# LSTM gates of one layer in one stationary block of 40 columns, and one gate row computed later

## The chip, the cores and the metric

The kernel runs on one core of a Trainium2 chip. The metric is the device time of one execution in microseconds (us). The kernel before took 2526.57, 2529.31 and 2533.30 us in three runs; the median is 2529.31 us.

## What is computed

A sequence of 256 positions with 1024 channels goes through a first block of two layers (band attention, short convolution, a gated feed-forward), and then through a second block of two layers. The first layer of the second block holds an mLSTM mixer, the second a stick-breaking attention, and both end in a "PEER" layer that picks 16 of 16384 experts for each of 8 heads and position and gathers their rows from memory. The change touches the gates of the mLSTM and the output gate of the first expert layer:

```
proj = einsum('bsd,de->bse', h, w_in)
qk, v, o, gates = split(proj, [1024, 2048, 3072])      # gates: 2 x 8 heads = 16 columns
gates = gates + b_if
i_pre, f_pre = split(gates, 2)                         # input gates, forget gates
log_f = log_sigmoid(f_pre);  b = cumsum(log_f)         # then the state and the decay of every head
...
sh1, sc1, g1, sh2, sc2, g2 = split(ada_mod(c), 6)      # per layer
x = x + g1 * mixer(h1)
x = x + g2 * peer_ffn(h2)                              # g2 of layer 0 is the gate row that moves
```

All arrays are float32.

## The kernel before, in words

Every engine has a program of its own, written out by hand, and the engines wait for each other on named semaphores. TensorE (PE) multiplies, VectorE (DVE) does most elementwise work, ScalarE (ACT) does activations, casts and copies out of PSUM, SyncE (SP) issues the weight loads, GpSimd (POOL) issues the gathers of expert rows. Nothing is scheduled by a planner at this place: the order of the work is the order of the code, and tables of small numbers say at which head or expert row an extra piece stands.

**The LSTM part.** The normed input is kept in two parts, `x_hi` and `x_lo` (the tiles `flo_b` and `hT_r` in the profile), and so are the weights; a product is three matmuls for each of 8 blocks of 128 channels (high by high, high by low, low by high). The gate weights are `wg`, split by ACT into `wg_hi` (L1734) and by DVE into `wg_lo` (`wg_r` in the profile, L2417). On PE the order is: values and queries and keys, then the gate product into bank `pr[0]` (twice 24 matmuls, input gates and then forget gates, each with 8 stationary columns), then four pieces of the output-gate product (`gate_piece`, 96 matmuls in line L647), then four small transposes of the gate rows (L1199) that wait for the semaphore `if_exp`, five matmuls that keep the engine at work (`idle_products_in`, L745), and then the heads, which wait for `gcol_ready`.

DVE meanwhile convolves queries and keys (`lstm_conv`), splits weights (`lower`, L1971), and when its program comes to L2451 it waits for the gate product (`if_full`), adds the biases into `gi` and `gf`, and runs the scans that give the cumulated decays. Behind the scans stand `lower(10)` and `lower(11)`, and behind these the copy `gcol` (L2473) that lets the heads begin.

**The heads.** In each of 8 heads PE multiplies `gM` (L1211) and scores (L1216, L1217), then one extra piece, and then the values of the head before (`lstm_values`, L1223 to L1225), which wait for `pl_ready`. DVE computes `Dt` (L2480) from the L1211 result and `Pl` (L2500); `Pl` is what the values wait for. The extra pieces are `PIECES_IN_HEADS` (halves of the output-gate product, in heads 0, 1, 2, 4) and `ROWS_IN_HEADS` (halves of gate rows: `gate_row_half`, four transposing matmuls in L1034, which ACT copies into `grows` in L1661, in heads 3, 5, 6, 7). Row 0 of `grows` is used first, right after the LSTM; row 1 gates the first expert layer and is read first in `finish(0)`, more than 350 us later (L2700).

**The first experts.** `experts_first` on PE interleaves queries and keys of both tiles with products of the gathered expert rows (`weighted`, L1269). After the keys of the second tile stand two gate rows, at expert rows 60 and 64 (`EARLY_GATES`, `LATE_ROWS`). An expert row goes this way: POOL issues its gather (L1915) when its place in a ring of ten is free, DMA brings 1 MB, DVE takes the dot product (L2672), ACT makes the weight and its diagonal (L1709, L1713, L1719, the tile `junk`), PE multiplies and frees the place.

Of the kernel before, what the change touches and what calls it, by code (L numbers as in the profile page):

```python
# [9 lines left out]
F32R = mybir.dt.float32r  # L10
I32 = mybir.dt.int32
U32 = mybir.dt.uint32
ALU = mybir.AluOpType
# [4 lines left out]
P = 128  # L18
D = 1024
SEQ = 256  # L20
NT = SEQ // P
KC = D // P
DEPTH = 2
# [13 lines left out]
COLS = 512  # L37
# [16 lines left out]
A_UNITS = 4 + 2 + 4 + 6 + 4 + 4 + 4 + 4 + 1  # L54
# [8 lines left out]
LSTM_HEADS, LSTM_QK, LSTM_V, LSTM_CONV = 8, 64, 128, 4  # L63
AHEAD = 4
WARM = {"begin": 14, "ffn input": 4, "lstm input": 11, "rotated columns": 7, "lstm gates": 5, "lstm output": 5}
PIECES_IN_HEADS = {0: (4, 0), 1: (4, 1), 2: (6, 0), 4: (6, 1)}
ROWS_IN_HEADS = {3: (0, 0), 5: (0, 1), 6: (1, 0), 7: (1, 1)}
GATE_ROWS = (2, 5, 11)
LATE_ROWS = ((2, 11), (0, 8))
SB_HEADS, SB_DIM = 16, 64  # L70
PEER_HEADS, NKEYS, TOPK = 8, 128, 16
EXPERTS = NKEYS * NKEYS
# [84 lines left out]


EARLY_COLUMNS = {(0, 2): (0, 0, 2, 4), (0, 3): (8, 10, 14, 16), (1, 2): (18, 20, 20, 24), (1, 1): (28, 30, 32, 34), (1, 3): (42, 44, 46, 48)}
ROWS_BACK, EARLY_KEYS, EARLY_GATES = 40, (50, 52, 54, 56), (60, 64)  # L160


def multiplied(k):
# [7 lines left out]
PEER_A_UNITS = 8 + 8 + 8 + 2  # L171
LSTM_A_UNITS = 6 + 4 + LSTM_HEADS + 4
TILE_A_UNITS = 10 + 2 + 2 + 4 + 4 + 4
A_BANKS = DEPTH * A_UNITS + 4 + LSTM_HEADS + 4

SLOTS_L, SLOTS_B, R2, SLOTS_T = 8, 12, 2, 12

# [20 lines left out]
def build(nc, ins, out):  # L198
    ctx = ExitStack()
    with ctx:  # L200
# [9 lines left out]
        def twice(name, shape, stack=ctx):  # L210

            with ExitStack() as once:
                plain = sb(name, shape, F32, once)
            return plain, sb(name + "_r", shape, F32R, stack)
# [84 lines left out]
        x_hi, x_lo = flo_b[:, :, :].rearrange("p k s -> p (k s)").rearrange("p (t k n) -> p t k n", k=KC, n=P), hT_r  # L299
# [6 lines left out]
        lstm = ExitStack()  # L306
        def sl(name, shape, dt=F32):
            return sb(name, shape, dt, lstm)
        biglm = sl("biglm", [P, 3 * P])
        wg, wg_lo = twice("wg", [P, KC, 2 * LSTM_HEADS], lstm)  # L310
        wg_hi = sl("wg_hi", [P, KC, 2 * LSTM_HEADS], F32R)
        bif = sl("bif", [LSTM_HEADS, 2])
        hng = sl("hng", [P, KC])
        preT = sl("preT", [P, KC, SEQ + LSTM_CONV - 1])
# [6 lines left out]
        gi, gf, ge, gl, gb_, gg, gM, gm, gone = [sl(n, [LSTM_HEADS, SEQ]) for n in  # L321
                                                 ("gi", "gf", "ge", "gl", "gb_", "gg", "gM", "gm", "gone")]
# [94 lines left out]
        pr = [psum(f"pr{i}") for i in range(4)]  # L417
# [221 lines left out]
        def _(pe):  # L639
# [6 lines left out]
            def mm(out_, lhsT, rhs, start, stop):  # L646
                m = nc.tensor.matmul(out_, lhsT, rhs, start=start, stop=stop)  # L647
                if not stop and owed[0]:
                    m.then_inc(w_free, 1)
                    owed[0] -= 1  # L650
                elif not stop and owed_half[0]:
                    m.then_inc(half_used, 1)
                    owed_half[0] -= 1
                return m
# [44 lines left out]
            def seq_of(v):  # L699

                return (lambda k: v[:, :, k, :]) if v is x_hi else (lambda k: v[:, k, 0:SEQ])
# [45 lines left out]
            for l in range(DEPTH):  # L747
# [33 lines left out]
                for t in range(NT):  # L781
                    for i in (Q_S, Q_S + 1):
                        b = bank_a()
                        for n in (2 * i, 2 * i + 1):
# [6 lines left out]
                            m = rows_product_late(b, n, tile_of(x_hi, t), tile_of(x_lo, t), arrived, lower_there)  # L791
# [4 lines left out]
                for n in (2 * KV_S, 2 * KV_S + 1):  # L796
                    split(n)
                    for t in range(NT):
                        m = rows_product(banks[t], n, tile_of(x_hi, t), tile_of(x_lo, t))
# [7 lines left out]
                for j in range(KC // 2):  # L807
# [4 lines left out]
                    for i in range(4):  # L812
                        c, t = 2 * j + i // 2, i % 2
                        m = nc.tensor.transpose(b[:, i * P:(i + 1) * P], zrow[:, t, c * P:(c + 1) * P], ident[:, :])
                    m.then_inc(pa_full, 1)
                for j in range(KV_HEADS // 2):
                    b = bank_a()
                    for i in range(4):
                        g, t = 2 * j + i // 2, i % 2
                        m = nc.tensor.transpose(b[:, i * P:(i + 1) * P], kdup[:, t, g].rearrange("p a d -> p (a d)"), ident[:, :])  # L820
# [62 lines left out]
                for j in range(KC // 2):  # L883
                    b = bank_a()
                    for i in range(4):
                        c, t = 2 * j + i // 2, i % 2
                        m = nc.tensor.transpose(b[:, i * P:(i + 1) * P], orow[:, t, c * P:(c + 1) * P], ident[:, :])
# [114 lines left out]
                for i in range(FFN_S + 1, DOWN_S):  # L1002
# [3 lines left out]
                    for n in (2 * i, 2 * i + 1):  # L1006
                        split(n)
                        for c in range(2):
                            if n % 2 == 0:
                                banks.append(bank_d())  # L1010
                            m = split_products(banks[c], n, c)
# [152 lines left out]
                i.then_inc(pd_full, 1)  # L1164
                half_done(m)
            pe.wait_ge(wg_ready, 1)
            for g in range(2):
                for k in range(KC):
                    for q, (w, h) in enumerate(((wg_hi, x_hi), (wg_hi, x_lo), (wg_lo, x_hi))):
                        m = mm(pr[0][0:LSTM_HEADS, g * SEQ:(g + 1) * SEQ], w[:, k, g * LSTM_HEADS:(g + 1) * LSTM_HEADS], seq_of(h)(k),  # L1170
                               k == 0 and q == 0, k == KC - 1 and q == 2)
            m.then_inc(if_full, 1)
            gate_bank = []

# [22 lines left out]
            for i in range(4):  # L1197
                src = (gg, gm)[i // 2]
                m = nc.tensor.transpose(pr[1][:, i * LSTM_HEADS:(i + 1) * LSTM_HEADS], src[:, (i % 2) * P:(i % 2 + 1) * P],  # L1199
                                        ident[0:LSTM_HEADS, 0:LSTM_HEADS])  # L1200
# [26 lines left out]
            for h in range(LSTM_HEADS + 1):  # L1227
                if h < LSTM_HEADS:
                    lstm_scores(h)
                if h in PIECES_IN_HEADS:  # L1230
                    gate_piece(*PIECES_IN_HEADS[h])
                if h in ROWS_IN_HEADS:
                    g, half = ROWS_IN_HEADS[h]
# [686 lines left out]
        def _(dve):  # L1920
# [135 lines left out]
            for l in range(DEPTH):  # L2056
# [175 lines left out]
                for j in range(4):  # L2232
# [5 lines left out]
                    w = sgb[:, c, :].rearrange("p c n -> p (c n)")  # L2238
# [72 lines left out]
                else:  # L2311
                    dve.wait_ge(cols2_in, 16)
                    for n in range(5):
                        c = KV_ADA + KC if n == 4 else ((n // 2) * 6 + 3 * (n % 2) + 1) * KC
                        g = N_KV if n == 4 else (N_MIX, N_FFN)[n % 2] + (n // 2) * KC
# [133 lines left out]
            before_conv(3)  # L2449
            dve.wait_ge(if_full, 1)  # L2450
            nc.vector.tensor_scalar(gi[:, :], pr[0][0:LSTM_HEADS, 0:SEQ], bif[:, 0:1], None, ALU.add)  # L2451
            nc.vector.tensor_scalar(gf[:, :], pr[0][0:LSTM_HEADS, SEQ:2 * SEQ], bif[:, 1:2], None, ALU.add)
            dve.drain()
            nc.vector.scalar_tensor_tensor(ge[:, :], gf[:, :], -1.0, gf[:, :], ALU.mult, ALU.max)
            dve.drain()
# [431 lines left out]
```

## Time and profile before

| | |
|---|---|
| median of three runs (2526.57 to 2533.30) | 2529.31 us |
| the profiled execution: span from the first to the last instruction | 2524.7 us |
| its own time | not recorded beside the span |
| PE busy | 2032.2 us (80%) |
| DVE busy | 1719.8 us (68%) |
| ACT busy | 955.0 us (38%) |
| POOL busy | 658.8 us (26%) |
| mean granted TensorE clock | 0.913 |

All times in rows are counted from the span's start. "Busy" adds up the durations of an engine's instructions; the durations of matmuls overlap, so that what one of many matmuls takes is read from the distance between starts, or from a run of them in the chain of waits. "Idle before" in square brackets is how long the engine stood before an instruction, with what ended the wait. The chain of waits is found by going back from the last instruction to what released it, again and again.

### The profile page before, as it was taken

How to read it: one execution, taken by the hardware profiler on the slowest of the kernel's cores; microseconds unless marked ns; L12 is line 12 of the kernel's file. 1: busy time of each engine (PE TensorE's matmuls, PEld its weight loads, DVE VectorE, ACT ScalarE, POOL GpSimd, SP SyncE). 2: the span in 40 equal slices, each digit the busy share in tenths (PEclk: the TensorE clock that was granted, in tenths of full speed). 3: DMA queues.
4: the chain of work that ended last, by engine and by line, in shares of the span. 5: the costliest groups of instructions: out<-in, count | busy, mean ns of one | idle time of the engine just before them, and what ended most of it. 6: DMA issues, size and time to landing. Idle time of an engine off the chain costs nothing.

```text
span 2524.7 us, 33890 instructions
## 1 busy us (share of the span) xinstructions
PE 2032.2 (80%) x12150; PEld 1384.9 (55%) x12150; DVE 1719.8 (68%) x3454; ACT 955.0 (38%) x2101; POOL 658.8 (26%) x631
## 2 busy tenths in 40 slices
PE   8999999999999999997665587777577778556555
PEld 7999899899989979874321123243122325211111
DVE  5687787768778867677588555558754757776544
ACT  4434533444544345432332224423223732322222
POOL 0000001000000100024445433344432335444442
PEclk9999999999999999999887798899788889887767
DMA  7545577674547763279999999999999999999998
GB/s 304 212 167 209 182 277 283 240 262 161 202 172 277 268 256 142 84 319 388 422 421 422 419 423 422 403 421 421 412 404 401 421 410 383 421 422 421 422 421 337
DMA packets 110947, 823.98 MB, mean 326 GB/s; under 512 B 14432, under 2 KB 15344, under 8 KB 31040
## 3 DMA queue, kind: packets, MB, share of 16 engines
q0 software_dynamic: 90000, 595.97, 57.8%
q1 hardware_dynamic: 20784, 225.89, 23.3%
q8 instruction: 96, 1.57, 0.2%
q14 instruction: 67, 0.55, 0.1%
HBM read 820.76 MB, written 1.05 MB: 326 GB/s over the span
## 4 chain that ended last, share of the span: by engine, by line
PE 47%; DMA 27%; DVE 11%; ACT 5%; issue 4%; POOL 2%; DVEq 2%; ACTq 1%; SPq 0%; POOLq 0%
DMA ring_b<-in_peer_uv,eidx 17%; PE pd L647 14%; PE pa L647 10%; PE pr L1269 9%; PE pr L647 7%; DMA wring<-in_peer_uv,eidx 6%; DVE wring_r L1971 2%; DVE ring_b L2672 2%; DMA ring_c<-in_peer_uv,eidx 1%; DVE wring L2672 1%; PE pa L1387 1%; ACT junk L1719 1%; POOL ring_b L1915 1%; PE pd L1292 1%; PE pa L1292 1%
## 5 line engine op out<-in xcount | busy, mean ns | idle before, releaser
L1269 PE MATMUL pr<-ring_b,junk 128*64 128x512 f32 x880 | 288.6, 765 | 156.5 <-ACT junk L1719 155.8
L1269 PE MATMUL pr<-wring,junk 128*64 128x512 f32 x840 | 269.4, 748 | 171.1 <-ACT junk L1719 170.6
L1915 POOL DMA_INDIRECT ring_b<-in_peer_uv,eidx x220 | 252.9, 1150 | 532.8 <-PE pr L1269 302.4
L2672 DVE CUSTOM_DVE_ANT_0 ring_b<-ring_b,hrow 128x1024 f32<-128x1024 f32 x220 | 267.9, 1224 | 180.9 <-DMA ring_b<-in_peer_uv,eidx 174.2
L2672 DVE CUSTOM_DVE_ANT_0 wring<-wring,hrow 128x1024 f32<-128x1024 f32 x210 | 255.4, 1223 | 187.8 <-DMA wring<-in_peer_uv,eidx 181.7
L1915 POOL DMA_INDIRECT wring<-in_peer_uv,eidx x210 | 247.8, 1180 | 332.6 <-PE pr L1269 277.3
L1709 ACT ACTIVATE gel<-dots 128x2 f32<-128x2 f32 x255 | 51.8, 203 | 654.4 <-DVE dots L2672 650.7
L1899 POOL DMA_DIRECT2D aring<-in_ada_rows x112 | 60.2, 538 | 840.9 <-DVE adal L2066 787.3
L1269 PEld LDWEIGHTS pr<-ring_b,junk 128*64 128x64 f32 x880 | 69.3, 165 | 350.8 <-ACT junk L1719 242.6
L1269 PEld LDWEIGHTS pr<-wring,junk 128*64 128x64 f32 x840 | 64.1, 159 | 345.6 <-ACT junk L1719 243.5
L1971 DVE TENSOR_TENSOR wring_r<-wring,wtop 128x2048 fp32r<-128x2048 f32 x76 | 171.7, 2261 | 54.7 <-ACT wtop L1431 52.4
L647 PE MATMUL pd<-hhi,wring_r 128*128 128x256 f32 x960 | 204.2, 281 | 0.0
L1971 DVE TENSOR_TENSOR wring_r<-wring,wring_r 128x2048 fp32r<-128x2048 f32 (+1 forms) x77 | 173.7, 2262 | 38.1 <-ACT wring_r L1431 35.7
L1431 ACT CAST wring_r<-wring 128x2048 fp32r<-128x2048 f32 x80 | 149.7, 1886 | 70.0 <-DMA wring<-in_w_mix 25.1
L1431 ACT CAST wtop<-wring 128x2048 fp32r<-128x2048 f32 x80 | 149.1, 1882 | 62.7 <-DMA wring<-in_w_back 24.4
L1269 PE MATMUL pr<-ring_c,junk 128*64 128x512 f32 x328 | 109.1, 754 | 75.1 <-ACT junk L1719 74.7
L647 PE MATMUL pa<-flo_b,wring_r 128*128 128x256 f32 x768 | 166.6, 283 | 0.0
L647 PEld LDWEIGHTS pd<-hhi,wring_r 128*128 128x128 f32 x960 | 158.6, 188 | 0.1
L1719 ACT ACTIVATE junk<-halves,gel 128x64 f32<-128x64 f32 x510 | 149.6, 340 | 17.8 <-issue 0.3
L2066 DVE CUSTOM_DVE_ANT_0 aring<-aring,crow 128x1024 f32<-128x1024 f32 x112 | 136.5, 1218 | 13.9 <-DMA aring<-in_ada_rows 12.6
L2672 DVE CUSTOM_DVE_ANT_0 ring_c<-ring_c,hrow 128x1024 f32<-128x1024 f32 x82 | 100.0, 1223 | 55.4 <-DMA ring_c<-in_peer_uv,eidx 53.5
L1713 ACT ACTIVATE gel<-gel,wexp 128x1 f32<-128x1 f32 x510 | 122.7, 287 | 18.8 <-issue 1.4
(441 smaller groups left out, 4566.4 us busy)
## 6 DMA issues: line engine op xcount, KB each, us to landing
wring<-in_w_mix SPq DMA_DIRECT2D x38, 2048.0 KB, 8.8
aring<-in_ada_rows POOLq DMA_DIRECT2D x112, 512.0 KB, 5.1
wring<-in_w_ffn SPq DMA_DIRECT2D x22, 2048.0 KB, 8.3
wring<-in_w_lstm SPq DMA_DIRECT2D x12, 2048.0 KB, 7.7
wring<-in_w_stick SPq DMA_DIRECT2D x12, 2048.0 KB, 11.7
wring<-in_w_back SPq DMA_DIRECT2D x8, 2048.0 KB, 8.1
ring_c<-in_w_stick SPq DMA_DIRECT2D x5, 2048.0 KB, 12.1
wring<-in_w_back SPq DMA_DIRECT2D x4, 1536.0 KB, 6.9
```

The costliest lines, as they stand in the source:

```text
L647: m = nc.tensor.matmul(out_, lhsT, rhs, start=start, stop=stop)
L1269: m = nc.tensor.matmul(pr[half][side, :], diag[:, p % DIAGS, :], row(p)[:, D + half * 512:D + (half + 1) * 512], start=p in FIRST_OF_SIDE, ...
L1292: i = nc.tensor.matmul(b[:, :], src(k), w(k), start=(k == 0), stop=(k == KC - 1))
L1431: nc.scalar.copy(hi, raw).then_inc(whi_ready, 1)
L1709: nc.scalar.activation(gel[:, p:p + PART], dots[:, p:p + PART], ACT.Gelu)
L1713: nc.scalar.activation(gel[:, i:i + 1], gel[:, i:i + 1], ACT.Copy, scale=wexp[:, g * PART // PICKS % NT, c // TOPK, c % TOPK:c % TOPK + 1])
L1719: nc.scalar.activation(diag[:, q % DIAGS, :], halves[:, :], ACT.Copy, scale=gel[:, q % PICKS:q % PICKS + 1]).then_inc(diag_ready, 1)
L1899: pool.dma_start(aring[:, a, :], ins["ada_rows"][bass.ds(2 * i + a, 1)].rearrange("a p n -> p (a n)")).then_inc(ada_in[a], 16)
L1915: pool.indirect_dma_start(out=row(q), out_offset=None, in_=ins["peer_uv"], in_offset=bass.IndirectOffsetOnAxis(ap=eidx[:, tt % NT, CHOSEN[ ...
L1971: nc.vector.tensor_tensor(lo, raw, hi, ALU.subtract).then_inc(wlo_ready, 1)
L2066: nc.vector.tensor_tensor_reduce(out=aring[:, j % 2, :], in0=aring[:, j % 2, :], in1=crow[:, :], scale=1.0, scalar=0.0, op0=ALU.mult, op1= ...
L2672: m = nc.vector.tensor_tensor_reduce(out=row(q)[:, 0:D], in0=row(q)[:, 0:D], in1=hrow[:, q // PICKS % NT, SIDE[q], :], scale=1.0, scalar=0 ...
```

## The change

The gate weights come as 40 columns instead of 16: 8 for the input gates, 24 zeros, 8 for the forget gates. One stationary block of 40 columns then gives both gates in 24 matmuls, and DVE reads the forget gates from partitions 32 to 39. The casts of the gate weights grow from 128 to 320 elements per partition, and their load from 64 KB to 160 KB. Gate row 1 leaves heads 6 and 7 and is computed in one piece behind expert row 68; since the list is worked off in order, it is row 1 that now stands at 60, row 2 at 64 and row 0 at 68.

```diff
-ROWS_IN_HEADS = {3: (0, 0), 5: (0, 1), 6: (1, 0), 7: (1, 1)}
+ROWS_IN_HEADS = {3: (0, 0), 5: (0, 1)}
-LATE_ROWS = ((2, 11), (0, 8))
+LATE_ROWS = ((1, 5), (2, 11), (0, 8))
+F_AT = 32
+GATE_COLS = F_AT + LSTM_HEADS
-ROWS_BACK, EARLY_KEYS, EARLY_GATES = 40, (50, 52, 54, 56), (60, 64)
+ROWS_BACK, EARLY_KEYS, EARLY_GATES = 40, (50, 52, 54, 56), (60, 64, 68)
-A_BANKS = DEPTH * A_UNITS + 4 + LSTM_HEADS + 4
+A_BANKS = DEPTH * A_UNITS + 4 + LSTM_HEADS + 2 * len({g for g, _ in ROWS_IN_HEADS.values()})
-        wg, wg_lo = twice("wg", [P, KC, 2 * LSTM_HEADS], lstm)
-        wg_hi = sl("wg_hi", [P, KC, 2 * LSTM_HEADS], F32R)
+        wg, wg_lo = twice("wg", [P, KC, GATE_COLS], lstm)
+        wg_hi = sl("wg_hi", [P, KC, GATE_COLS], F32R)
-            for g in range(2):
-                for k in range(KC):
-                    for q, (w, h) in enumerate(((wg_hi, x_hi), (wg_hi, x_lo), (wg_lo, x_hi))):
-                        m = mm(pr[0][0:LSTM_HEADS, g * SEQ:(g + 1) * SEQ], w[:, k, g * LSTM_HEADS:(g + 1) * LSTM_HEADS], seq_of(h)(k),
-                               k == 0 and q == 0, k == KC - 1 and q == 2)
+            for k in range(KC):
+                for q, (w, h) in enumerate(((wg_hi, x_hi), (wg_hi, x_lo), (wg_lo, x_hi))):
+                    m = mm(pr[0][0:GATE_COLS, 0:SEQ], w[:, k, :], seq_of(h)(k), k == 0 and q == 0, k == KC - 1 and q == 2)
-            nc.vector.tensor_scalar(gf[:, :], pr[0][0:LSTM_HEADS, SEQ:2 * SEQ], bif[:, 1:2], None, ALU.add)
+            nc.vector.tensor_scalar(gf[:, :], pr[0][F_AT:GATE_COLS, 0:SEQ], bif[:, 1:2], None, ALU.add)
-    sent["w_gates"] = a["ma_w_in_2"][0, :, 6 * COLS:]
+    gates = a["ma_w_in_2"][0, :, 6 * COLS:]
+    sent["w_gates"] = np.concatenate([gates[:, :LSTM_HEADS], np.zeros((D, F_AT - LSTM_HEADS), np.float32), gates[:, LSTM_HEADS:]], axis=1)
```

On PE, in heads 6 and 7, the kernel before has these rows (head 6 from its L1211 to the values of head 5, and the same again for head 7):

```order
L1211 MATMUL pr0<-gM,ident 128x256 [waits m_read]
L1216 MATMUL pr2<-qkT 128x256 [waits st_read]
L1217 MATMUL pr2<-qkT 128x128
L1034 MATMUL pa1<-ident,adac 128x128 [waits pa_free]
L1034 MATMUL pa1<-ident,adac 128x128 x3
L1223 MATMUL pa0<-vaug,Pl 128x129 [waits pa_free,pl_ready]
L1224 MATMUL pa0<-vaug,Pl 128x129
L1225 MATMUL pa0<-vaug,Pl 128x129
```

The changed kernel has at the same place:

```order
L1211 MATMUL pr0<-gM,ident 128x256 [waits m_read]
L1216 MATMUL pr2<-qkT 128x256 [waits st_read]
L1217 MATMUL pr2<-qkT 128x128
L1223 MATMUL pa1<-vaug,Pl 128x129 [waits pa_free,pl_ready]
L1224 MATMUL pa1<-vaug,Pl 128x129
L1225 MATMUL pa1<-vaug,Pl 128x129
```

The half gate row is gone from between the scores and the values, and the values take the other bank of the pair.

On ACT, after the keys of the second tile, the kernel before goes on like this behind the gate row at expert row 64 (`gel` and `junk` are the weights and diagonals of expert rows, two rows at a time):

```order
L1661 COPY grows<-pa 128x512 [waits pa_full] x2
L1709 ACTIVATE gel<-dots 128x2 [waits dots_ready]
L1713 ACTIVATE gel<-gel,wexp 128x1 x2
L1719 ACTIVATE junk<-halves,gel 128x64 [waits rows_free] x2
L1709 ACTIVATE gel<-dots 128x2 [waits dots_ready]
L1713 ACTIVATE gel<-gel,wexp 128x1 x2
L1719 ACTIVATE junk<-halves,gel 128x64 [waits rows_free] x2
L1709 ACTIVATE gel<-dots 128x2 [waits dots_ready]
```

In the changed kernel, from the same place on:

```order
L1661 COPY grows<-pa 128x512 [waits pa_full] x2
L1709 ACTIVATE gel<-dots 128x2 [waits dots_ready]
L1713 ACTIVATE gel<-gel,wexp 128x1 x2
L1719 ACTIVATE junk<-halves,gel 128x64 [waits rows_free] x2
L1709 ACTIVATE gel<-dots 128x2 [waits dots_ready]
L1713 ACTIVATE gel<-gel,wexp 128x1 x2
L1719 ACTIVATE junk<-halves,gel 128x64 [waits rows_free] x2
L1661 COPY grows<-pa 128x512 [waits pa_full] x2
L1709 ACTIVATE gel<-dots 128x2 [waits dots_ready]
```

Two more copies, which wait for a third gate row on PE, stand ahead of the weights of expert rows 68 and 69.

## Rows read from the trace of the kernel before

**Rows 1.** The page: mean busy share of the DMA engines in 40 slices.
```profile
DMA  7545577674547763279999999999999999999998
```
**Rows 2.** Stretches: busy time and count of each engine, granted clock, DMA share, GB/s.
```profile
1000.00:1020.00 20.00, 19.78 (x145) 17.65 (x144) 14.62 (x21) 10.88 (x16) 0.00 (x0) 1.00 0.28 106
...
1180.00:1200.00 20.00, 12.11 (x74) 7.04 (x72) 13.78 (x49) 5.57 (x21) 10.43 (x10) 1.00 1.01 420
...
1280.00:1300.00 20.00, 15.07 (x58) 5.71 (x60) 19.00 (x80) 7.71 (x29) 9.91 (x8) 1.00 1.01 421
```
**Rows 3.** Chain of waits, 988 to 1012 us: start, duration, what.
```profile
990.88 5.46 PE pr L647 x48
996.34 11.51 PE pd L647 x96
...
1008.48 1.31 PE pr L745 x10
```
**Rows 4.** Groups of weight loads (PEld), 990.5 to 996.2 us: count, busy, mean ns.
```profile
L647 PEld LDWEIGHTS pr<-flo_b,wg_hi 128*8 128x8 f32 x16 | 1.4, 88 | 0.4
L647 PEld LDWEIGHTS pd<-wring_r,flo_b 128*128 128x128 f32 x2 | 0.3, 188 | 0.0
```
**Rows 5.** DVE in order of time, 974 to 1009 us: start, duration, instruction, idle before.
```profile
974.99 0.29 DVE L2417 TENSOR_TENSOR wg_r<-wg,wg_hi 128x128 fp32r<-128x128 f32 x1 [0.40 <-ACT wg_hi L1734]
...
995.37 0.68 DVE L2424 COPY preT<-pd 128x512 f32<-128x512 f32 x1
996.38 0.47 DVE L2451 TENSOR_SCALAR gi<-pr,bif 8x256 f32<-8x256 f32 x1 [0.33 <-PE pr L647]
...
1004.47 4.49 DVE L1971 TENSOR_TENSOR wring_r<-wring,wtop 128x2048 fp32r<-128x2048 f32 x2
1008.88 0.18 DVE L2473 TENSOR_SCALAR gcol<-pr 128x32 f32<-128x32 f32 x1
```
**Rows 6.** ACT in order of time, 974 to 1005 us.
```profile
974.67 0.29 ACT L1734 CAST wg_hi<-wg 128x128 fp32r<-128x128 f32 x1
976.13 1.92 ACT L1431 CAST wring_r<-wring 128x2048 fp32r<-128x2048 f32 x1 [1.17 <-DMA wring<-in_w_lstm]
...
1004.41 0.42 ACT L1746 ACTIVATE gm<-gm 8x256 f32<-8x256 f32 x1 [1.09 <-DVEq L2468]
```
**Rows 7.** PE and DVE in order of time, heads 6 to 8, 1032 to 1039 us.
```profile
1032.81 1.16 PE L1034 MATMUL pa<-ident,adac 128*128 128x128 f32 x8
1033.85 0.49 PE L1223 MATMUL pa<-vaug,Pl 128*128 128x129 f32 x2
...
1038.45 0.49 PE L1223 MATMUL pa<-vaug,Pl 128*128 128x129 f32 x2 [0.30 <-DVEq L2502]
...
1032.07 0.74 DVE L2480 SCALAR_TENSOR_TENSOR Dt<-pr,gcol,biglm 128x256 f32<-128x256 f32 x2 [1.27 <-PE pr L1211]
1033.11 0.56 DVE L2500 SCALAR_TENSOR_TENSOR Pl<-pr,Dt 128x384 f32<-128x384 f32 x1 [0.30 <-PE pr L1217]
...
1037.71 0.56 DVE L2500 SCALAR_TENSOR_TENSOR Pl<-pr,Dt 128x384 f32<-128x384 f32 x1 [0.16 <-issue]
```
**Rows 8.** PE at expert rows 60 to 72; DMA issues, 1255 to 1315 us, median to landing.
```profile
1276.42 2.05 PE L1034 MATMUL pa<-ident,adac 128*128 128x128 f32 x16
1280.21 7.08 PE L1269 MATMUL pr<-wring,junk 128*64 128x512 f32 x16 [1.75 <-ACT junk L1719]
...
1294.98 1.94 PE L1269 MATMUL pr<-ring_c,junk 128*64 128x512 f32 x8
...
ring_b<-in_peer_uv,eidx POOLq DMA_INDIRECT x9, 14.3
```
**Rows 9.** Two pauses of PE in order of time, and the clock inside the second.
```profile
1185.27 1.94 PE L1269 MATMUL pr<-ring_c,junk 128*64 128x512 f32 x8 [2.93 <-ACT junk L1719]
...
1245.17 4.24 PE L1269 MATMUL pr<-wring,junk 128*64 128x512 f32 x5 [5.97 <-ACT junk L1719]
...
1244.00:1246.00 2.00, 0.83 (x1) 0.29 (x2) 0.00 (x0) 1.22 (x5) 0.00 (x0) 0.50 1.05 446
```

## The prediction, made before the changed kernel was run

> **What bounds the kernel now.** I read the page's slices first. From about the 19th of 40 slices to the end the DMA row reads 9 in every slice but the last, so the second half is bound by the gather of expert rows [rows 1]; around expert rows 60 to 70 the share is 1.01 at 421 GB/s [rows 2]. In that half an instruction more on PE or ACT costs nothing as long as gathers are always queued, and whatever comes earlier in the first half moves the whole second half forward by the same amount. The first half at the place of the change is the LSTM stretch, with PE at 19.78 of 20 us, the clock at 1.00 and DMA at 0.28 [rows 2]. The chain of waits runs through PE there: the 48 gate matmuls, the 96 of the four pieces, the transposes, the warming matmuls, and the first head [rows 3]. So a reader of the chain alone would credit every microsecond taken from PE. The orders in time of DVE and ACT beside it [rows 5, 6] show how far the other engines were behind, and that decides.
>
> **Gate product, on PE.** 48 matmuls took 5.46 us, 113.8 ns each [rows 3]. Half of them go. With 24 left at the same distance the block takes 2.73 us; at the distance of the 128-column products behind it (11.51 us for 96, 119.9 ns) [rows 3] it takes 2.88 us. Taken: 2.6 us saved, both ends within 0.1 us. PE then finishes the four pieces at 1007.85 - 2.65 = 1005.2 (996.34 + 11.51 = 1007.85).
>
> Wider stationary blocks also take longer to load: 88 ns with 8 columns, 188 ns with 128 [rows 4]; a straight line between them gives about 115 ns for 40, and a load of 188 ns already hides behind matmuls 119.9 ns apart. The Trainium skill says that the time of a weight load scales with its column count ("TensorE: Matmul & The Clock Gate", section "Step-by-step: what each phase is for"), which speaks against the wider block. If the 27 ns more were all exposed, 24 of them would take back 0.65 us; the trace agrees that wider loads are longer, but not that they are exposed.
>
> **Gate product, on DVE.** Here the gain meets its first limit. DVE had waited only 0.33 us for the gate product; it had come out of its own work at 995.37 + 0.68 = 996.05 [rows 5]. The scans behind that wait cannot start more than 0.33 us earlier. And DVE gets later: the two splits of the gate weights grow from 128 to 320 elements. DVE needs 2.245 us for 2048 and 0.29 for 128, 1.02 ns an element, so 192 more cost 0.20 us [rows 5]; ACT needs 1.92 and 0.29, 0.85 ns an element, so 0.16 us [rows 6]. DVE waited for that cast (0.40 us idle before L2417) and hardly stood still from there to 996.05, so both fall on it: 0.36 us. It is then ready at 996.41, with the usual gap of about 0.1 us at 996.5, against 996.38 before. The scans start 0.1 us later, not 2.6 us earlier. ACT itself is covered: behind its cast it waited 1.17 us for a weight load [rows 6].
>
> **The first new wait.** The transposes wait for `if_exp`, given by the ACT row that ended at 1004.83 [rows 6], now about 1004.95; PE arrives at 1005.2, just late enough. Behind them the warming matmuls end at 1009.79 - 2.65 = 1007.1 (1008.48 + 1.31 = 1009.79 before [rows 3]). The heads wait for `gcol_ready`. Before, `gcol` ended at 1008.88 + 0.18 = 1009.06, in time. Now it is behind the same DVE work, `lower(10)` and `lower(11)` with 4.49 us [rows 5], and ends at about 1009.2. With the hand-over from DVE to PE of 0.18 us (1037.71 + 0.56 = 1038.27 to 1038.45 [rows 7]) the first head starts at 1009.4 instead of 1009.8. What stays of 2.6 us is 0.4 us; PE stands for 2.2 us in front of the heads. Behind the waiting L1211 all the heads are queued, so nothing else fills the time. Bounds: 0 (if the DVE delay is 0.4 us larger than worked out) and 0.8 us (if none of the 0.36 us lands on DVE).
>
> **Half gate rows out of heads 6 and 7.** PE spent 1.16 us on each, 1.04 us from its start to that of the next instruction (1032.81 to 1033.85) [rows 7], and the chain ran through one of them. But the values behind them wait for `Pl`: in head 6 `Pl` ran from 1033.11 to 1033.67, and the values began at 1033.85, 0.18 us later [rows 7]. In head 8, where no half row stands and PE is seen waiting for DVE, the distance from the end of `Pl` to the values is the same 0.18 us. So the half row filled a pause of PE, and it goes out of a place where it cost nothing. `Pl` itself hangs on `Dt` at 1032.07, and that on L1211, ahead of the half row. The ACT copies were not waited for by anything but the ring. Gain 0; bounds 0 and 0.1 us a head.
>
> **The third gate row at expert row 68.** PE gets 16 matmul passes, 2.05 us, and ACT two copies. When the same stood at row 60, PE began it at 1276.42 and resumed products at 1280.21, 3.8 us later [rows 8]. At row 68 the products of ring_c at 1294.98 followed without a pause, so they would come up to 3.8 us later, and two places are freed so much later once; after that PE has pauses to catch up. A gather lands 14.3 us after its issue in this stretch [rows 8], while 1 MB at 421 GB/s takes 2.5 us, so several are always queued, and 3.8 us do not empty the queue. Cost 0; bounds 0 and 3.8 us. I take 0, since the same piece at rows 60 and 64 left the DMA share at 1.01 [rows 2].
>
> **The load of the gate weights** grows by 96 KB. It lies in a stretch where the DMA engines are far from full, and is issued tens of microseconds ahead of its use; 0.
>
> **Sum.** -0.4 (heads start earlier) + 0 + 0 + 0 = -0.4 us on the profiled execution: 2524.7 becomes 2524.3 us of span. The median of the runs lies 4.6 us above that span (2529.31 - 2524.7), and I carry this over: 2528.9 us.
>
> **Rivals.**
> A, PE time counts in full: the block gives 2.7 us and each half row 1.04 us, 4.8 us together, 2524.5 us. For it speaks the chain, which runs through all of these on PE. Against it speak the 0.33 us of DVE and the 0.18 us behind `Pl` [rows 5, 7]. Chance 0.08.
> B, the pause of 2.2 us before the heads lowers the clock of PE. After a pause of 5.97 us the clock was at 0.50, that is 1.2 GHz [rows 9]. If it stayed low for some 7 us in the heads, PE would lose up to 3.5 us: 2532.4 us. Against it: a pause of 2.93 us lies in a stretch with the clock at 1.00, 2.4 GHz [rows 2, 9], and the new one is shorter and follows solid work. The Trainium skill has idle gaps that take the clock down ("TensorE: Matmul & The Clock Gate", section "HAM oscillation — how this bites in real kernels"); this trace agrees for the long pause only. Chance 0.03.
> C, the place where the change turns slower: ACT holds the weights of expert rows 68 and 69 behind the copies, POOL cannot issue, and the gather queue runs dry. That costs what exceeds the queue, at most 3.8 us: -0.4 + 3.8 = +3.4, 2532.7 us. It decides only from a queue shorter than 3.8 us; 14.3 us to landing speak against it. Chance 0.05.
> D, the change does not do what it says: a matmul with 40 columns is slower, or the forget gates at partition 32 cost DVE more. Up to the 2.2 us of new pause the first is hidden, the second would add tenths: 2529.4 us. Chance 0.04.
> The forecast itself has 0.80.
>
> **How the numbers follow.** What can be told from no change in this kernel is about 0.3%, 7.6 us, that is below 2521.7 or above 2536.9 us. No case reaches either bound; only the scatter of runs (6.7 us between the lowest and the highest of three) could. So faster by over 0.3% has 0.05, within 0.3% 0.92, slower 0.03. The range reaches from below rival A, 2523.5, to above rival C, 2533.5 us; it also holds all three runs of the kernel before.
>
> **What would show it.** In the changed profile: 24 gate matmuls in about 2.8 us; no idle time of DVE before `gi`, at about 996.5; `gcol` at about 1009.0 and a PE wait of some 2 us before the first L1211, ended by DVE; the first L1211 at 1009.4; the values of heads 5 and 6 again 0.18 us behind `Pl`, with heads 6 and 7 as long as before (3.4 us); a third L1034 group near 1295 us and a DMA share of 1.0 around it. The prediction is wrong if `gi` starts earlier than 996.1, if heads 6 and 7 shorten by more than 0.2 us, or if the DMA share drops between 1295 and 1320 us.

## The result and the profile after

The changed kernel is slower: 2533.80 us median (2528.74 to 2548.00, 12 runs) against 2528.17 us (2525.07 to 2533.31, 12 runs) for the kernel before on the same chip. The ratio is 1.0025, 95% interval 1.0015 to 1.0036. The difference of the two means is 6.5 us, with a standard error of 1.8. The prediction was 2528.9 us with a range up to 2533.5; the measured median lies 0.3 us above that range, and 5.6 us above the kernel before. The loss is shown, since the interval is above 1, but it is 0.25%, not over the 0.3% that the prediction named as the bound. The scatter has grown too: 19 us between the lowest and the highest run, against 8 us.

The profiled execution of the changed kernel took 2542.66 us, with a span of 2541.0 us. It is one of the two slowest of the twelve, so its sizes are those of a bad execution; its order and its places are what is read from it.

Up to the heads it is nearly what was forecast. DVE in order of time (start, duration, instruction, idle before):

```profile
975.21 0.49 DVE L2417 TENSOR_TENSOR wg_r<-wg,wg_hi 128x320 fp32r<-128x320 f32 x1 [0.56 <-ACT wg_hi L1734]
...
996.57 0.47 DVE L2451 TENSOR_SCALAR gi<-pr,bif 8x256 f32<-8x256 f32 x1
...
1004.77 4.49 DVE L1971 TENSOR_TENSOR wring_r<-wring,wtop 128x2048 fp32r<-128x2048 f32 x2
1009.30 0.19 DVE L2473 TENSOR_SCALAR gcol<-pr 128x32 f32<-128x32 f32 x1
```

These answer to [rows 5]: the split of the gate weights is longer, `gi` no longer waits, and `gcol` comes 0.4 us later. PE in order of time, at the end of the pieces, in head 0 and in heads 6 to 8 (line 647 of before is L649 here, line 745 is L747, line 1034 is L1036):

```profile
990.89 0.28 PE L649 MATMUL pr<-flo_b,wg_hi 128*40 128x256 f32 x1
...
993.69 0.40 PE L649 MATMUL pd<-wring_r,flo_b 128*128 128x256 f32 x2
...
1006.00 1.38 PE L747 MATMUL pr<-ident 128*128 128x128 f32 x10
1009.58 1.21 PE L1211 MATMUL pr<-gM,ident 8*128 8x256 f32 x2 [2.20 <-DVEq L2474]
1010.71 1.22 PE L1216 MATMUL pr<-qkT 64*128 64x256 f32 x2
...
1044.48 0.69 PE L1211 MATMUL pr<-gM,ident 8*128 8x256 f32 x2
1045.11 0.70 PE L1216 MATMUL pr<-qkT 64*128 64x256 f32 x2
1045.64 0.38 PE L1217 MATMUL pr<-qkT 64*128 64x128 f32 x2
1046.99 0.67 PE L1223 MATMUL pa<-vaug,Pl 128*128 128x129 f32 x2 [0.97 <-DVEq L2502]
...
1048.45 1.22 PE L1211 MATMUL pr<-gM,ident 8*128 8x256 f32 x2
```

The 24 gate matmuls take 993.69 - 990.89 = 2.80 us. The pause in front of the first head is 2.20 us, as forecast, and it ends at 1009.58 us. But the L1211 behind it takes 1.21 us, and one of a later head (head 6, at 1044.48) 0.69 us. The stretches of the trace say why (busy time and count of PE, PEld, DVE, ACT and POOL, then the granted clock, the DMA share, GB/s):

```profile
1000.00:1020.00 20.00, 17.58 (x94) 14.82 (x93) 12.68 (x18) 9.61 (x11) 0.00 (x0) 0.74 0.28 105
1020.00:1040.00 20.00, 20.00 (x71) 16.14 (x71) 7.29 (x13) 4.86 (x19) 0.00 (x0) 0.50 0.00 1
1040.00:1060.00 20.00, 18.71 (x93) 15.74 (x93) 9.06 (x29) 10.04 (x33) 0.00 (x0) 0.74 0.00 1
1060.00:1080.00 20.00, 18.57 (x157) 18.23 (x156) 13.61 (x32) 9.92 (x21) 0.00 (x0) 1.00 0.29 106
...
1008.00:1010.00 2.00, 0.42 (x1) 0.43 (x2) 1.46 (x2) 1.81 (x3) 0.00 (x0) 0.90 0.98 418
1010.00:1012.00 2.00, 2.00 (x6) 1.16 (x5) 0.74 (x2) 0.37 (x1) 0.00 (x0) 0.50 0.97 418
...
1038.00:1040.00 2.00, 2.00 (x11) 2.00 (x11) 0.26 (x1) 0.00 (x0) 0.00 (x0) 0.50 0.00 0
1040.00:1042.00 2.00, 2.00 (x12) 1.55 (x12) 0.16 (x1) 0.79 (x5) 0.00 (x0) 0.92 0.00 0
1042.00:1044.00 2.00, 2.00 (x15) 1.75 (x15) 1.43 (x4) 0.86 (x4) 0.00 (x0) 1.00 0.00 0
...
1046.00:1048.00 2.00, 1.03 (x6) 1.01 (x6) 0.85 (x2) 0.69 (x2) 0.00 (x0) 0.79 0.01 4
1048.00:1050.00 2.00, 2.00 (x6) 1.12 (x6) 0.29 (x1) 0.90 (x5) 0.00 (x0) 0.50 0.00 0
```

Where the kernel before had 1.00 in the stretch of the first head [rows 2], the clock is at 0.50, that is 1.2 GHz, from the pause to about 1040 us. Added up from the stretches of 2 us, the spell lasts 30.7 us. PE is 20.00 of 20 us busy from 1020 to 1040 and yet only 71 instructions fall into them, where the kernel e4 below, with the clock at 1.00, has 122. The busy share hides the loss; the clock column and the count show it. A second fall follows the pause of 0.97 us in head 6, where the values of head 5 wait for `Pl`: that is the pause that the half gate row had filled. This spell lasts some 10 us.

To say where the time went, I take two marks in each profile: the start of `gi` on DVE, and the first transposing matmul after the heads (L1248, `y_columns`). The second mark, first in the kernel before and then in the changed one:

```profile
1045.81 1.06 PE L1248 MATMUL pa<-ident,xn 128*128 128x128 f32 x8 [0.37 <-issue]
...
1062.22 1.06 PE L1248 MATMUL pa<-ident,xn 128*128 128x128 f32 x8 [0.37 <-issue]
```

Between the marks the kernel before takes 49.43 us (from 996.38), the changed one 65.65 us (from 996.57). That is 16.2 us, and the spans differ by 2541.0 - 2524.7 = 16.3 us. So all the rest of these two executions adds up to nearly nothing. That each part of the rest kept its time is not shown by this. In the experts the third gate row (its 16 passes, then the stretch around them) leaves the DMA share at 1.01:

```profile
1309.70 2.05 PE L1036 MATMUL pa<-ident,adac 128*128 128x128 f32 x16
...
1300.00:1320.00 20.00, 15.64 (x73) 7.64 (x71) 19.84 (x85) 8.29 (x27) 9.23 (x9) 1.00 1.01 420
```

### The profile page after: what moved, and what is told of

Its sections match the earlier page's. It is cut to its first block, busy times and chain, and to the rows that moved or that the text cites. A ratio compares the mean times of both kernels' runs of the same rounds, so it can differ in the third digit from the quotient of the medians.

```text
span 2541.0 us, 33842 instructions
## 1 busy us (share of the span) xinstructions
PE 2056.1 (81%) x12126; PEld 1399.8 (55%) x12126; DVE 1722.5 (68%) x3454; ACT 954.8 (38%) x2101; POOL 648.2 (26%) x631
## 3 DMA queue, kind: packets, MB, share of 16 engines
HBM read 820.85 MB, written 1.05 MB: 323 GB/s over the span
## 4 chain that ended last, share of the span: by engine, by line
PE 42%; DMA 29%; DVE 12%; ACT 5%; issue 5%; POOL 2%; DVEq 2%; ACTq 1%; PEld 0%; PEldq 0%; POOLq 0%; SPq 0%
DMA ring_b<-in_peer_uv,eidx 18%; PE pd L649 13%; PE pa L649 9%; DMA wring<-in_peer_uv,eidx 8%; PE pr L1269 8%; PE pr L649 5%; DVE wring_r L1971 2%; DVE ring_b L2672 2%; POOL ring_b L1915 1%; ACT junk L1719 1%; PE pa L1292 1%; PE pa L1387 1%; DMA aring<-in_ada_rows 1%; DVE wring L2672 1%; POOL wring L1915 1%
## 5 line engine op out<-in xcount | busy, mean ns | idle before, releaser
L1269 PE MATMUL pr<-wring,junk 128*64 128x512 f32 x840 | 284.0, 781 | 161.8 <-ACT junk L1719 159.6
L1915 POOL DMA_INDIRECT ring_b<-in_peer_uv,eidx x220 | 247.1, 1123 | 544.0 <-PE pr L1269 294.2
L649 PE MATMUL pd<-hhi,wring_r 128*128 128x256 f32 x960 | 204.3, 281 | 0.0
L649 PE MATMUL pa<-flo_b,wring_r 128*128 128x256 f32 x768 | 166.5, 283 | 0.0
L649 PEld LDWEIGHTS pd<-hhi,wring_r 128*128 128x128 f32 x960 | 158.7, 189 | 0.1
```

The costliest lines, as they stand in the source:

```text
L1269: m = nc.tensor.matmul(pr[half][side, :], diag[:, p % DIAGS, :], row(p)[:, D + half * 512:D + (half + 1) * 512], start=p in FIRST_OF_SIDE, ...
L1915: pool.indirect_dma_start(out=row(q), out_offset=None, in_=ins["peer_uv"], in_offset=bass.IndirectOffsetOnAxis(ap=eidx[:, tt % NT, CHOSEN[ ...
```

## The experiments

Differences are those of the means of a kernel's runs and of the kernel before on the same chip, in us, with the standard error. "Marks" is the distance between the two marks in the one profiled execution, "pause" the idle time of PE before the first L1211 there. The experiments ran on three chips: one for e1 to e4, one for e5 to e8, one for e9 to e12. The kernel before itself had a median of 2526.35, 2529.10 and 2528.31 us on them.

| run | block of 40 | rows out of heads | warming | pause | marks | difference | ratio, 95% interval |
|---|---|---|---|---|---|---|---|
| before | no | no | 5 | 0 | 49.43 | 0 | |
| after | yes | yes | 5 | 2.20 | 65.65 | +6.5 ± 1.8 | 1.0025 (1.0015 to 1.0036) |
| e1_block_only | yes | no | 5 | 2.20 | 62.35 | +7.7 ± 1.0 | 1.0030 (1.0020 to 1.0041) |
| e9_pause_alone | no | no | 0 | 2.08 | 63.43 | +6.8 ± 1.6 | 1.0021 (1.0009 to 1.0033) |
| e4_block_filled | yes | no | 13 | 0.41 | 49.04 | -2.5 ± 0.9 | 0.9989 (0.9980 to 0.9998) |
| e10_block_filled_again | yes | no | 13 | 0.42 | 49.09 | +1.5 ± 0.7 | 1.0004 (0.9995 to 1.0013) |
| e7_extra_gate_row | yes | no, and a third row at 68 | 13 | 0.42 | 49.09 | -0.6 ± 0.7 | 0.9995 (0.9986 to 1.0004) |
| e11_extra_row_again | yes | no, and a third row at 68 | 13 | 0.39 | 49.11 | +0.3 ± 0.8 | 0.9998 (0.9990 to 1.0007) |
| e6_gcol_earlier | yes | no | 5 | 0 | 47.32 | -2.7 ± 0.7 | 0.9988 (0.9979 to 0.9997) |
| e8_before_unwarmed | no | no | 0 | 0.67 | 50.33 | +0.3 ± 1.2 | 0.9999 (0.9989 to 1.0008) |
| e2_rows_only | no | yes | 5 | 0 | 51.15 | +2.1 ± 1.0 | 1.0008 (0.9998 to 1.0018) |
| e3_after_filled | yes | yes | 13 | 0.41 | 51.18 | +2.4 ± 1.1 | 1.0011 (1.0000 to 1.0021) |
| e5_all_filled | yes | yes, filled | 13 | 0.38 | 49.04 | +0.3 ± 0.9 | 0.9999 (0.9989 to 1.0008) |
| e12_after_gcol_earlier | yes | yes | 5 | 0 | 49.24 | +1.0 ± 0.7 | 1.0001 (0.9992 to 1.0010) |

The standard errors hold only for the scatter of runs on one chip. e4 and e10 are one and the same kernel on two chips, and they differ by 4.0 us against the kernel before, over three standard errors. So a difference of under some 4 us between kernels on different chips is not to be read from this table. The marks repeat far better, as long as the clock stays up: e4, e5, e7, e10 and e11 lie between 49.04 and 49.11 us, on three chips.

Several expectations below missed. e1 lost more than the 2 to 6 us expected; e3 and e5 did not come out as fast as expected, and e4 came out faster; e9 lost 6.8 us where 8 to 10 were expected; e10 was to repeat the gain of e4 and did not. e7 and e11 also lie a little outside what the theory gave them. What decides below is where the clock fell and where it did not.

**One part at a time.** The block of 40 columns with the rows left in heads 6 and 7, and the rows taken out with the old gate product:

```diff
# e1_block_only: the changed kernel with
-ROWS_IN_HEADS = {3: (0, 0), 5: (0, 1)}
+ROWS_IN_HEADS = {3: (0, 0), 5: (0, 1), 6: (1, 0), 7: (1, 1)}
# (and LATE_ROWS, EARLY_GATES as before); e2_rows_only: the kernel before with the other half of the change
```

> The 40-column gate block alone; the half gate rows stay in heads 6 and 7 and no third gate row stands in the experts. Theory (the pause in front of the heads lets the clock fall): PE again stands 2.2 us before the first L1211, and in part of the executions the granted clock is 0.50 for tens of microseconds in the heads. The median is then 2 to 6 us above the kernel before, and the spread of the runs wider. Rival 1 (the pauses in heads 6 and 7, where the half rows are gone, do it): the kernel is as fast as before or 0.4 us faster. Rival 2 (the third gate row in the experts costs the time): the same, 0.4 us faster than before.

> The old gate product (48 matmuls of 8 columns), only the half gate rows moved from heads 6 and 7 to expert row 68. Theory: PE has no pause in front of the heads, the clock stays at 1.00 up to head 6; the pauses of about 1 us in heads 6 and 7 are short, so within 1.5 us of the kernel before. Rival 1: low clock from head 6 on, some 2 to 6 us slower. Rival 2: slower by up to 3.8 us with a clock of 1.00 in all heads and a DMA share below 1 near expert row 70.

e1 alone loses as much as the full change, as far as the runs can tell: +7.7 ± 1.0 against +6.5 ± 1.8. By the marks it has 12.9 of the 16.2 us. Its stretches:

```profile
1000.00:1020.00 20.00, 17.57 (x96) 14.82 (x95) 12.68 (x19) 10.25 (x12) 0.00 (x0) 0.76 0.28 105
1020.00:1040.00 20.00, 20.00 (x71) 16.14 (x71) 7.85 (x13) 4.86 (x19) 0.00 (x0) 0.50 0.00 1
1040.00:1060.00 20.00, 19.25 (x130) 16.57 (x129) 9.07 (x29) 11.85 (x35) 0.00 (x0) 0.97 0.01 2
```

The same fall in front of the heads, with the same spell of 30.7 us, and no second one behind it: heads 6 and 7 kept their half rows and their clock. In e2 there is no pause before the heads, and only the second fall is seen. PE in heads 6 and 7, and then two stretches of 2 us:

```profile
1033.64 0.38 PE L1217 MATMUL pr<-qkT 64*128 64x128 f32 x2
1034.99 0.49 PE L1223 MATMUL pa<-vaug,Pl 128*128 128x129 f32 x2 [0.97 <-DVEq L2502]
...
1036.87 1.22 PE L1216 MATMUL pr<-qkT 64*128 64x256 f32 x2
1037.88 0.63 PE L1217 MATMUL pr<-qkT 64*128 64x128 f32 x2
...
1034.00:1036.00 2.00, 1.03 (x8) 0.89 (x8) 0.85 (x2) 0.73 (x3) 0.00 (x0) 1.00 0.02 4
1036.00:1038.00 2.00, 2.00 (x5) 1.17 (x6) 0.74 (x2) 1.08 (x6) 0.00 (x0) 0.51 0.00 0
```

A pause of 0.97 us, and the next scores take 1.22 us where they took 0.70. By the marks it costs 51.15 - 49.43 = 1.7 us; the runs say +2.1 ± 1.0, which by itself is not told from nothing.

**The pause filled.** Eight more warming matmuls in front of the heads, useless work in a place where PE stands anyway, in the full change (e3) and in the block alone (e4):

```diff
-WARM = {"begin": 14, "ffn input": 4, "lstm input": 11, "rotated columns": 7, "lstm gates": 5, "lstm output": 5}
+WARM = {"begin": 14, "ffn input": 4, "lstm input": 11, "rotated columns": 7, "lstm gates": 13, "lstm output": 5}
```

> The changed kernel with 13 instead of 5 warming matmuls in front of the heads, 8 times 0.26 us = 2.1 us, which fill the new pause of 2.2 us and add nothing to the path. Theory: the clock stays at 1.00 up to the heads, the median falls back to that of the kernel before or 0.4 us below it (-0.4 to +1 us). Rival 1: the pauses in heads 6 and 7 are still there, so most of the 5.6 us stays. Rival 2: all of the 5.6 us stays.

> The 40-column block with 13 warming matmuls and the half rows in heads 6 and 7 as before. Theory: the clock is 1.00 through all heads, 0.4 us faster than before (between -1 and +0.5 us). If it is faster than e3 by over 1 us, the pauses in heads 6 and 7 have a share of their own; rival 1 expects just that. Rival 2 expects this one equal to e1 and both faster than e3.

PE of e4 at the same place, and the stretches of its heads:

```profile
1007.91 3.17 PE L747 MATMUL pr<-ident 128*128 128x128 f32 x26
1011.49 0.69 PE L1211 MATMUL pr<-gM,ident 8*128 8x256 f32 x2 [0.41 <-DVEq L2474]
...
1000.00:1020.00 20.00, 19.36 (x141) 17.17 (x140) 15.47 (x24) 12.36 (x18) 0.00 (x0) 1.00 0.29 106
1020.00:1040.00 20.00, 19.50 (x122) 15.74 (x121) 11.30 (x24) 10.64 (x37) 0.00 (x0) 1.00 0.00 0
```

Against e1, on the same chip, this is 10.2 ± 1.2 us less in the runs and 62.35 - 49.04 = 13.3 us less by the marks. The heads start no earlier (`gi` to L1211 is 13.0 us in both); only what PE does in the pause is changed. So the loss is the pause's effect on the clock and no property of the block. e3, the full change with the same filling, lies 4.9 ± 1.2 us above e4 in the runs and 2.1 us by the marks. The marks show the second fall again; the runs would leave room for more.

**All pauses filled, and the third gate row by itself.**

```diff
# e5_all_filled: e3, and in lstm heads 6 and 7, where the half rows stood
+                if h in (6, 7):
+                    pe.wait_ge(pd_free, nd[0] + 1)
+                    idle_products_in(pd[nd[0] % 2], 4)
# ...
# e7_extra_gate_row: e4, and (with the count of PSUM banks that belongs to it)
-LATE_ROWS = ((2, 11), (0, 8))
+LATE_ROWS = ((1, 5), (2, 11), (0, 8))
-ROWS_BACK, EARLY_KEYS, EARLY_GATES = 40, (50, 52, 54, 56), (60, 64)
+ROWS_BACK, EARLY_KEYS, EARLY_GATES = 40, (50, 52, 54, 56), (60, 64, 68)
```

> The changed kernel (third gate row at expert row 68, no half gate rows in heads 6 and 7) with 13 warming matmuls in front of the heads and 4 more, 1.0 us, in each of heads 6 and 7 in the place of the half row. Theory (every loss is the clock after a pause of PE): clock 1.00 through all heads, and as fast as e4: 2 to 3 us faster than before. Rival (the third gate row in the experts costs by itself): the clock is 1.00 too, but the time is 3 to 5 us above e4.

> e4 with a third gate row at expert row 68 added, row 1 being computed twice: the work in the experts alone is tested, with the heads of e4. Theory: the gather queue hides it, equal to e4 within 1 us. Rival: 2 to 4 us slower than e4, with the DMA share below 1 near 1300 us.

> The kernel of e4 once more (block of 40 columns, 13 warming matmuls, rows in the heads as before), on the chip of the next run: again 2 to 3 us under the kernel before. It is the base for the next run.

> The kernel of e7 once more: that of the run before plus a third gate row at expert row 68 (row 1 is computed twice, in the heads and there). Theory 'a third gate row in the experts is free': the same as the run before within 1 us. Rival 'it costs some': 1.5 to 3.5 us more than the run before, as e7 against e4 had 1.9 with a standard error of 1.1. The two pairs together decide at about 0.7 us.

With the half rows' place filled by four idle products each, the marks of the full change are at 49.0 us, as in e4: 2.1 us less than e3. That is the second fall taken back by useless work alone. What e5 still has over e4 in the runs, 2.8 ± 1.3 us, could be the third gate row, but the two ran on different chips. The two pairs made for it do not agree: e7 against e4 +1.9 ± 1.1, across two chips, and e11 against e10 -1.2 ± 0.9, on one chip. The pair on one chip is the one to read, and it shows no cost; the plain mean of both is +0.3 ± 0.7 us. A cost of 1 us is not excluded.

**The pause removed, not filled.** If DVE does `gcol` before `lower(11)`, PE has hardly anything to wait for. e6 is e1 with this, e12 the changed kernel with this:

```diff
             lower(DEPTH, 10)
-            lower(DEPTH, 11)
             dve.wait_ge(gcol_full, 1)
...
             decay(0)
+            lower(DEPTH, 11)
```

> The 40-column block, half rows in the heads as before, 5 warming matmuls; DVE does gcol ahead of lower(11), and lower(11) behind the first decay. gcol then ends near 1007.4, PE arrives at 1007.1: the pause is under 0.5 us and the heads start 2 us earlier than with the block alone. Theory: clock 1.00 in the heads and 2 to 5 us faster than before, faster than e4 by up to 2 us. Rival (the block itself slows the heads, not the pause): about as slow as e1, 7 us above before.

> The whole changed kernel with gcol ahead of lower(11) on DVE, as in e6, so that PE hardly stands before the first L1211; the half rows are out of heads 6 and 7. If the pause before the heads is all of the loss: at or 1 to 3 us under the kernel before, like e6. If the pauses in heads 6 and 7 and the third gate row take their own share: 2 to 5 us above e6, that is about 0 to 2 us above the kernel before, with a clock under 1.00 somewhere between 1030 and 1050 us.

PE of e6, in order of time:

```profile
1007.52 1.38 PE L747 MATMUL pr<-ident 128*128 128x128 f32 x10
1008.84 0.69 PE L1211 MATMUL pr<-gM,ident 8*128 8x256 f32 x2
1009.46 0.70 PE L1216 MATMUL pr<-qkT 64*128 64x256 f32 x2
```

Counted from `gi`, the first head starts 10.8 us later instead of 13.4 as before, and PE does not stand. The marks are at 47.3 us, 2.1 us under the kernel before, and the runs 2.7 ± 0.7 us under it. This is where the matmuls taken out of the gate product come to be worth something: the order of DVE had held them back. It is the best version tried by the marks, but its gain in the runs is within what the same kernel differed by on two chips (e4, e10), so it is not shown to beat the kernel before. The kernel before with only `gcol` moved was not run; little is to be expected of it, since there `gcol` ended at 1009.06 and PE came to the heads after it, at 1009.73. e12, the same with the rows out of heads 6 and 7, has marks of 49.2 us. The fall in heads 6 and 7 is there again (stretches of 2 us):

```profile
1032.00:1034.00 2.00, 1.03 (x7) 0.84 (x6) 0.85 (x2) 0.71 (x2) 0.00 (x0) 0.90 0.01 4
1034.00:1036.00 2.00, 2.00 (x5) 1.18 (x5) 0.66 (x2) 0.90 (x5) 0.00 (x0) 0.50 0.00 0
```

It takes back 1.9 of the 2.1 us. Three kernels with the rows out and the place empty (e2, e3, e12) have it in their profile, as the full change has; where the half rows stand or idle products fill their place, it is absent.

**A pause in the kernel before.** First the warming matmuls away, which leaves a pause of 0.67 us (e8), then a longer one by useless work on DVE (e9):

```diff
-"lstm gates": 5
+"lstm gates": 0
# e9_pause_alone only, ahead of gcol on DVE
+            for i in range(4):
+                nc.vector.tensor_scalar(Dt[:, i % 2, :], biglm[:, :], 0.0, None, ALU.add)
+                if i % 2:
+                    dve.drain()
```

> The kernel before without the five warming matmuls in front of the heads: PE pauses about 0.9 us there (it waits for gcol, which was ready 0.7 us before the last of them ended) and the heads start 0.5 us earlier. Theory: what counts is how long PE stands; a pause of 0.9 us is shorter than that of 2.2 us, so low clock is rarer: between 0.5 us faster and 3 us slower than before. Rival (any pause at this place is enough): 7 us slower, as e1.

> The kernel before, without its 5 warming matmuls in front of the heads and with 4 copies of 384 elements on DVE (of no use) ahead of gcol, so that PE stands some 2 us before its first L1211 though the gate product is the old one. Both theories: the heads start 1 to 2 us later than before, since DVE is the engine that is late. Theory 'the pause lowers the clock': on top of that the heads run at a granted clock of 0.50 for some tens of us, 8 to 10 us more than before in all. Rival 'it is the block of 40 columns itself (its wider loads, the forget gates at partition 32)': only the 1 to 2 us of the delay, clock at 1.00 in the heads.

PE of e9 before the first head, then its stretches:

```profile
1010.74 0.26 PE L1199 MATMUL pr<-ident,gm 8*128 8x8 f32 x2
1013.09 1.22 PE L1211 MATMUL pr<-gM,ident 8*128 8x256 f32 x2 [2.08 <-DVEq L2478]
...
1000.00:1020.00 20.00, 17.69 (x112) 15.47 (x111) 12.79 (x24) 11.05 (x12) 0.00 (x0) 0.82 0.29 107
1020.00:1040.00 20.00, 20.00 (x69) 16.14 (x70) 9.03 (x13) 4.86 (x19) 0.00 (x0) 0.50 0.00 1
```

With the old gate product of 48 matmuls and a pause of 2.08 us the same spell of 0.50 is there, 30.7 us again, with marks of 63.43 us and +6.8 ± 1.6 us in the runs. From `gi` to the first L1211 it takes 14.2 us where the kernel before took 13.4; this delay of 0.85 us is all that the slower DVE explains. The rival "the block of 40 columns itself" falls. In e8, with 0.67 us, the clock dips for a few microseconds only, the marks are 0.9 us longer than before, and the runs show nothing.

**One pause, with and without a fall.** All fourteen profiles (before, after, e1 to e12) hold a pause of 1.96 us at one place among the first expert rows, behind the same 16 matmul passes. In the kernel before and then in e2 (PE in order of time, then the stretch behind the pause, which is of 2 us):

```profile
1117.64 3.22 PE L1269 MATMUL pr<-ring_b,junk 128*64 128x512 f32 x7 [1.96 <-ACT junk L1719]
1118.00:1120.00 2.00, 2.00 (x6) 0.69 (x5) 1.44 (x7) 0.00 (x0) 0.00 (x0) 1.00 1.02 426
...
1120.48 4.92 PE L1269 MATMUL pr<-ring_b,junk 128*64 128x512 f32 x7 [1.96 <-ACT junk L1719]
1122.00:1124.00 2.00, 2.00 (x4) 0.50 (x3) 1.52 (x5) 0.00 (x0) 0.00 (x0) 0.50 1.00 418
```

The same seven matmul passes (x7) take 3.22 us in one and 4.92 us in the other. Of the fourteen profiles four show the fall there (e2, e5, e6, e7) and ten do not, with the same work and the same pause. So at this place neither decides alone: it differs from one execution to the next, by something that the program does not show. In front of and inside the heads it looks different. All eight pauses of 0.67 us or more there that began at 1.00 were followed by a fall within 3.2 us of their start. The pause of 1.05 or 1.06 us right behind the heads, which every profile has, was followed by none in the next 50 us. Why these places differ was not tested.

## Why the prediction was wrong

**The clock of PE after the pause (rival B): this is the step that failed.** The prediction saw the pause, its place and its length (2.2 us in the text, 2.20 in the profile), and named the fall of the clock as what it could do. It gave it 0.03, because a pause of 2.93 us lies in a stretch with the clock at 1.00 [rows 9]. One pause without a fall in one execution was taken as proof. It stands among the expert rows, where the work ahead and behind is another, and where a pause of 1.96 us brings the clock down in four profiles of fourteen; so it could speak neither for the heads nor for every execution. The sum had no term for the clock at all. Three kernels with a pause of 2.1 to 2.2 us there (after, e1, e9) fell to 0.50, and lost 6.5 to 7.7 us in the mean of the runs; filling it (e3, e4, e5) or reordering it away (e6, e12) kept 1.00 in the first head. None of the signs that the prediction named for being wrong came up (`gi` before 996.1, shorter heads 6 and 7, a lower DMA share): none of them looked at the clock.

**The size of B.** The prediction took a spell of some 7 us and up to 3.5 us of loss. The profiles show 30.7 us of spell and 13 to 16 us of loss by the marks, of which the difference of the means shows 6 to 8 us. The profiled executions of after and e9 are among the slowest two of twelve, so the spell may be shorter in the other ones; but that of e1, third of eight, has the same spell. How its length is distributed was not measured, since the other runs leave no stretches of the clock. e1's profiled execution took 2535.49 us, 9.1 us over the median of before, while its marks are 12.9 us longer (62.35 - 49.43); part of it may be given back later, and this too stays open.

**Half gate rows out of heads 6 and 7, "gain 0; bounds 0 and 0.1 us a head".** Right that nothing is gained, and for the reason given: the values wait for `Pl`, and 0.97 us of pause stand where 1.04 us of work stood. Wrong in that the bound stopped at zero on the other side. The row was the work that kept the clock up. The Trainium skill has a case near this one ("TensorE: Matmul & The Clock Gate", section "A second HAM failure mode: psum-queue depth-cycling"): frequent short idles of PE between groups of matmuls make its clock go down and up again. The traces of e2, e3 and e12 agree that short idles can do it, but here one pause of 0.97 us in head 6 came first, not a train of them. Removing the half rows costs 1.7 (e2 against before), 2.1 (e3 against e4) and 1.9 us (e12 against e6) by the marks.

**What held.** The gate product: 2.80 us, forecast 2.73 to 2.88. `gi` at 996.57, forecast 996.5; no idle time before it. The weight loads of 40 columns took 114 ns, where the straight line gave about 115. `gcol` at 1009.30, forecast 1009.0. The first L1211 at 1009.58, forecast 1009.4; it started 0.15 us earlier than before and not 0.4. For that there are two reasons: `gcol` came 0.3 us later than worked out, and before, L1211 started at 1009.73, not at the 1009.8 that the sum took from the end of the warming matmuls. That the pause of 2.2 us came out to the digit is in part luck: PE arrived 0.3 us later than forecast too (1006.00 + 1.38 = 1007.38, not 1007.1). The third gate row at 68: DMA share 1.01, and no cost in the pair on one chip. Rival A falls: no kernel gained 4.8 us. Rival C falls with the DMA share. Rival D falls with the 2.80 us and with e4's marks, which lie 0.4 us under those of before. Of the sum, -0.4 us was -0.15; what was missing is the term for the clock.

## What to carry to other kernels

When an edit takes work from PE in front of a wait that another engine ends, the work turns into a pause, and the pause can cost several times its length through the granted clock: here 2.2 us cost 13 to 16 us in the profiled executions and 6 to 8 us in the mean of the runs, and 0.97 us about 2 us. Not every pause does, and one profile in which the clock stayed up does not clear a pause: the one of 1.96 us among the expert rows had a fall in four profiles of fourteen. Before such an edit, look at what ends the wait; either move the other engine's instruction forward in the same step (here `gcol` before one `lower`), or leave or put cheap matmuls in the pause. After it, read the clock column of the stretches and the count of instructions, since the busy share of PE rises when the clock falls.

## What the runs showed of the hardware

- A pause of 2.20 us brought the granted clock from 1.00 to 0.50 for 30.7 us (after and e1; e9 the same with 2.08 us), though PE was busy 20.00 of 20 us in the middle of it. The pause of 2.93 us of [rows 9] did not lower it, nor did that of 1.06 us behind the heads in any profile. One of 1.96 us among the expert rows lowered it in four profiles of fourteen, with the same work around it. A pause of 0.97 us in the heads lowered it for about 7 us in e2, e3 and e12 and for 10 us in the changed kernel. In e8 0.67 us were followed by a dip (0.50 from 1014 to 1016 us, 0.98 in the next stretch of 2 us). So here the length of the pause alone decides neither the fall nor its length, and among the expert rows the work around it does not either; what does was not found.
- At 0.50 the scores take 1.22 us and not 0.70, the values 0.64 and not 0.39.
- Weight loads took 88 ns with 8 columns, 114 ns with 40 and 188 ns with 128; at 40 columns the matmuls stood 2.80 / 24 = 0.117 us apart, against 0.114 us with 8, so the longer load was almost wholly hidden.
- Eight useless matmuls saved 10.2 ± 1.2 us (e4 against e1) and started the heads no later.
- One kernel differed by 4.0 us against the kernel before between two chips (e4, e10), while both intervals reach only about 2.3 us to either side.
